# Two attention stages: half of the scaling of each head's probabilities goes from VectorE to ScalarE

## The reference

```python
s = jnp.einsum('...gnqd,...nkd->...gnqk', qb, kc, preferred_element_type=jnp.float32) * SCALE
s = jnp.where(mask, s, -jnp.inf)
m = jnp.max(s, axis=-1)
...
p = jnp.exp(s - m[..., None])
den = jnp.sum(p, axis=-1)
...
o = jnp.einsum('...gnqk,...nkd->...gnqd', p, vc.astype(jnp.float32)) / den[..., None]
```

## Time and profile before

| | |
|---|---|
| time, median of 3 runs | 998.2 us (994.24, 998.2, 1003.98) |
| span of the profiled execution | 996.8 us (its own time is not given apart from the span) |
| PE busy | 913.4 us (92%) |
| DVE busy | 655.8 us (66%) |
| ACT busy | 493.0 us (49%) |
| POOL busy | 81.1 us (8%) |

### The profile page before, as it was taken

How to read it: one execution, slowest core, us unless ns; L and a number is a source line. 1 busy time by engine, 2 the same in 40 slices (tenths; PEclk the granted TensorE clock), 3 DMA queues, 4 the chain that set the end, 5 groups by cost and what they waited for, 6 DMA issues and landing times. The chain is left out here.

```text
span 996.8 us, 14710 instructions
## 1 busy us (share of the span) xinstructions
PE 913.4 (92%) x5572; PEld 774.3 (78%) x5572; DVE 655.8 (66%) x1221; ACT 493.0 (49%) x902; POOL 81.1 (8%) x87
## 2 busy tenths in 40 slices
PE   4897779999999999999999999998988789889887
PEld 3785447899998878776799999886887468668755
DVE  4778994655555458876755556447876947787454
ACT  5444662545454335476554555334544635455651
POOL 2000000000000000000000000004643000220010
PEclk9998979999999999999999999999998999999799
DMA  9464003566656647523656656657752026533101
GB/s 332 141 204 168 1 1 113 163 190 191 192 189 210 189 152 216 174 94 107 177 171 189 200 173 212 190 154 199 242 177 95 1 69 201 169 106 118 52 1 43
DMA packets 96790, 148.69 MB, mean 149 GB/s; under 512 B 6272, under 2 KB 59680, under 8 KB 96592
## 3 DMA queue, kind: packets, MB, share of 16 engines
q1 hardware_dynamic: 94512, 140.50, 44.8%
q10 hardware_dynamic: 1296, 4.83, 1.5%
q0 software_dynamic: 912, 2.41, 0.9%
HBM read 146.67 MB, written 1.05 MB: 148 GB/s over the span
## 5 line engine op out<-in xcount | busy, mean ns | idle before, releaser
L1025 DVE TENSOR_TENSOR w_lo<-w_raw,w_hi 128x1024 fp32r<-128x1024 f32 (+2 forms) x269 | 319.9, 1211 | 139.3 <-ACT w_hi L618 135.7
L618 ACT ACTIVATE w_hi<-w_raw 128x1024 fp32r<-128x1024 f32 (+2 forms) x269 | 274.4, 1042 | 152.6 <-DMA w_raw<-in_w_gate_up 61.4
L1731 PE MATMUL ps<-hT_hi,w_lo 128*128 128x256 f32 x704 | 199.6, 284 | 2.5 <-DVE w_lo L1025 1.9
L1732 PE MATMUL ps<-hT_hi,w_hi 128*128 128x256 f32 x704 | 199.2, 283 | 0.0
L1733 PE MATMUL ps<-hT_lo,w_hi 128*128 128x256 f32 x704 | 199.2, 283 | 0.0
L1731 PE MATMUL ps<-w_hi,hT_lo 128*128 128x512 f32 (+3 forms) x448 | 174.2, 389 | 11.1 <-DVE w_lo L1025 4.4
L1733 PE MATMUL ps<-w_lo,hT_hi 128*128 128x512 f32 (+3 forms) x448 | 170.4, 380 | 0.0
L1732 PE MATMUL ps<-w_hi,hT_hi 128*128 128x512 f32 (+3 forms) x448 | 170.1, 380 | 0.0
L1731 PEld LDWEIGHTS ps<-hT_hi,w_lo 128*128 128x128 f32 x704 | 135.1, 192 | 3.2 <-ACT z L687 2.1
L1732 PEld LDWEIGHTS ps<-hT_hi,w_hi 128*128 128x128 f32 x704 | 135.1, 192 | 0.0
L1733 PEld LDWEIGHTS ps<-hT_lo,w_hi 128*128 128x128 f32 x704 | 135.1, 192 | 0.0
(11 more groups left out here) (239 smaller groups left out, 1189.6 us busy)
## 6 DMA issues: line engine op xcount, KB each, us to landing
w_raw<-in_w_gate_up SPq DMA_DIRECT2D x176, 256.0 KB, 4.4
w_raw<-in_w_down SPq DMA_DIRECT2D x44, 512.0 KB, 4.2
w_raw<-in_w_in_e SPq DMA_DIRECT2D x38, 512.0 KB, 4.7
w_raw<-in_w_qkv_o SPq DMA_DIRECT2D x24, 512.0 KB, 4.3
w_raw<-in_w_in_o SPq DMA_DIRECT2D x20, 512.0 KB, 3.7
w_raw<-in_w_out_e SPq DMA_DIRECT2D x16, 512.0 KB, 4.9
w_raw<-in_w_out_o SPq DMA_DIRECT2D x16, 512.0 KB, 3.5
w_raw<-in_w_in_e SPq DMA_DIRECT2D x8, 268.0 KB, 2.7
```

What stands on the lines that cost most here:

```text
L618: n.activation(w_hi[:, u % RING, 0:size], w_raw[:, u % RING, 0:size], ACT.Copy).then_inc(hi_ready, 1)
L1025: v.tensor_tensor(w_lo[:, u % RING, 0:size], w_raw[:, u % RING, 0:size], w_hi[:, u % RING, 0:size].bitcast(F32), ALU.subtract).then_inc(lo ...
L1731: m.matmul(o, lhs[1], rhs[0], start=start, stop=False)
L1732: m.matmul(o, lhs[0], rhs[0], start=False, stop=False)
```

## The change

In `attn0` and `attn2` DVE no longer scales tile 0. It increments a new semaphore `fac_ready`, with an instruction of its own, once `fac` is written, and scales tile 1 as before. ACT scales tile 0 of head `s-1` in step `s`, behind the exponents of head `s`, with a copy whose scale is the column of `fac`, and signals `half_ready`. The transposes of a head wait for `probs_ready` and `half_ready`. `attn1` and `attn3` are left as they are: their own functions on ACT and PE do not take part, and `scale_probs` keeps L1264 for them.

```diff
@@ ScalarE, attention, behind the exponents of head s
+                j = s - 1
+                if 0 <= j < len(inst):
+                    i, w = i0 + j, P if inst[j]["causal"] else T
+                    act.wait_ge(sem("fac_ready"), (i if stage == "attn0" else len(INST["attn0"]) + j) + 1)
+                    n.activation(prob[:, i % 4, 0:w], prob[:, i % 4, 0:w], ACT.Copy, scale=fac[:, i, 0:1])\
+                     .then_inc(sem("half_ready"), 1)
                 j = s - LAG
@@ VectorE, scale_probs
             w = P if it["causal"] else T
-            v.tensor_scalar(prob[:, i % 4, 0:w], prob[:, i % 4, 0:w], fac[:, i, 0:1], None, ALU.mult)
+            if stage in ("attn0", "attn2"):
+                dve.sem_inc(sem("fac_ready"), 1)
+            else:
+                v.tensor_scalar(prob[:, i % 4, 0:w], prob[:, i % 4, 0:w], fac[:, i, 0:1], None, ALU.mult)
             v.tensor_scalar(prob[:, i % 4, 256:512], prob[:, i % 4, 256:512], fac[:, i, 1:2], None, ALU.mult)\
              .then_inc(probs_ready, 1)
@@ TensorE, transposed
             pe.wait_ge(probs_ready, i + 1)
+            if stage in ("attn0", "attn2"):
+                pe.wait_ge(sem("half_ready"), (i if stage == "attn0" else len(INST["attn0"]) + j) + 1)
```

## The result

The changed kernel takes 1006.3 us (median of 20 runs, 1000.9 to 1010.4), the kernel before on the same chips 1002.7 us (20 runs, 994.2 to 1005.7). The ratio is 1.0047, with a 95% interval of 1.0028 to 1.0065: about 4.7 us slower, where 0.6 us faster was forecast. The 8.7 us between the forecast of 997.6 and the measured 1006.3 have three parts: 4.5 are the kernel before itself, whose median over 20 runs lies above the 998.2 of the three runs shown ahead; 3.6 are the change, by the medians; 0.6 is the gain that did not come.

What follows compares the result with a forecast made beforehand. DVE was taken as the bound in most of attn0 and in attn2 from about head 6; -0.9 us for attn0 and +0.3 for attn2 gave -0.6, so 997.6 us, with a range of 992.8 to 1003.

Steps and rivals of the forecast that it cites:

- What bounds the kernel now: DVE's list bounds attn0 except at the start (4.42 us a pair), and attn2 from about head 6 until the last four.
- What DVE is spared: Scaling of tile 0 leaves DVE: 24 x 0.20 us in attn0 and 16 x 0.26 in attn2, 9.0 us.
- What DVE is given: The separate increment costs DVE about 0.11 us, 40 times: 4.4 us, leaving a net saving of 4.6 us.
- What ACT is given: Scaling copies on ACT of 0.40 us in attn0 and 0.49 in attn2, 17.4 us in all; ACT does not become the bound.
- What becomes later: Transposes in attn0 start 2.02 us into a head, 0.47 later; a pair saves 0.18 at full clock, loses 0.13 at half.
- Sum for `attn0`: Start +0.25 us, ten pairs -1.5 with one at half clock, end +0.4: together -0.9 us.
- Sum for `attn2`: Start +0.79 us, heads 4 to 12 save 1.2, some 0.6 of latency in the last four heads: +0.3 us.
- Rival B: PE stays at half clock; some seven more pairs of attn0 each lose 0.31 to 1 us: 1002 us, chance 0.15.
- Total: Whole kernel: -0.9 + 0.3 = -0.6 us, 996.2 against the profiled 996.8, so 997.6 for the median of runs.
- nothing downstream moves: Behind the changed stages no time changes: the next projection's weight units are ready two steps ahead, no DMA issue moves.
- A: DVE's saving lands whole: -9.0 us, 989.2; with the increment's price and only the latency hidden -4.6, 993.6; chance 0.11.
- C: Latency bounds every pair of attn2: 0.71 us for each of 8 pairs, +4.8 us in total, 1003; chance 0.08.

Runs made afterwards that it cites:

- the folded kernel: The changed kernel with the fac_ready increment put on the last instruction that writes fac, everything else the same; ratio 0.9991 to the kernel before.
- the earliest transposes, between the exponents: The changed kernel with the increment on fac's last instruction and ACT scaling tile 0 of head s-1 between head s's two exponents; ratio 1.0008 to the kernel before.

## Why the prediction was wrong

**"What bounds the kernel now", "What DVE is spared", "What DVE is given": right.** A pair of `attn0` saves 0.16 to 0.17 us in the trace (4.42 to 4.26; over all the pairs that DVE paces 0.15 to 0.17) for the 0.18 forecast; a pair of `attn2` 0.29 (5.04 to 4.75) for 0.30, in the two pairs from head 8 to 12. From head 6 to 8 it is 0.15. The increment costs 0.11 us, measured by itself.

**"What ACT is given", "What becomes later": right in a pair.** The new rows last 0.39 and 0.50 us, ACT is no bound, and the transposes begin 2.05 us into the head for 2.02. One thing was off by 0.05 us: from ACT's end to PE's start it takes 0.10 us, where I carried over the 0.05 from DVE's end to PE's start.

**"Sum for `attn0`", "Sum for `attn2`": the ends right in latency, wrong in clock.** +0.4 for the end of `attn0` was 0.38 at equal clock. The last four heads of `attn2` were given +0.7 in two parts (from -0.4 to +0.3); 0.31 from head 12 to 15 and 0.42 in the tail make 0.73. The start of `attn0`, +0.25, was 0.38 from head 0 to 4 (7.39 to 7.77 us), at half clock in both. But "by the trace's clock one of them at half clock" assumed that the changed kernel would meet the clock of the one profile I had. It did not. In the profiled execution the tail of `attn0` grew by 2.4 us and that of `attn2` by 2.0, of which 2.0 and 1.5 are half clock; the pair before the tail of `attn0` lost 0.42 instead of gaining 0.18. Over four profiles a side the tails grew by 1.4 and 1.9. The terms for the ends, +0.4 and +0.6, are the ones that were too small: this is the step that failed. Rival B's mechanism came true, in places that I had not looked at. Why the clock falls there is not explained by it.

**Rival B** put the price on seven pairs inside `attn0`, decided by a PEclk below 0.75, and was given 0.15. PEclk of `attn0` only went from 0.81 to 0.76 (means over four profiles: 0.80 to 0.77), and the pairs in the middle kept their saving. The loss was in the tails, where one clock level costs the whole chain of transposes, copy and values, in single pairs at half clock near both ends of `attn0` (4.83 for 4.41, 5.61 for some 4.5), and beyond them in dense products, which PE bounds. I had also said why B was not my forecast: PE's total idle time shrinks. In `attn0` it did not grow much (57.3 - 42.9 = 14.4 us before, 15.1 after), and the clock fell all the same. The Trainium skill, "TensorE: Matmul & The Clock Gate", Part 1, ties the clock to PE's idleness; the runs with PE kept busy agree, with 62.9 us at half clock down to 45.3. A total over the stage did not tell; what would have, no run shows.

**"Total", "nothing downstream moves".** The output projection behind `attn0` waits for no weight unit in either kernel, but the clock moved, and the 45 us behind `attn0` went from 1.0 to 3.9 us at half clock, which costs 2 us each time (35.0 to 37.0).

**The size.** At equal clock the change measures +1.2 ± 0.4 us where the sum said -0.6. The 0.30 us for a us at half clock is an average over all places; in dense products and in a tail it is more (1.5 us in the tail of `attn2`, for 2 x 0.22 x 7.78 = 3.4 us at half clock). If the extra half-clock time lies in such places, as the four profiles suggest, a price near 0.45 makes 11.5 us worth 5.2, and the rest -0.6, the same as the forecast. That is an argument, not a measurement, and one result speaks against it: by the same price the folded kernel stands at -0.6 too, so that 40 increments would cost nothing at equal clock, where the increment alone comes to 2.4. How the 4.6 us divide between clock and latency is known to about 1.5 us.

**What stays open.** Why PE falls to half clock more often with the change. It is not the last head's transposes (1.0055 without them), and it is tied to the increment in some way (62.3 us at half clock without it, 74.4 with), yet the earliest transposes, between the exponents, brought it back to 71.4. With errors of 2.4 to 3.1 us on each of these means, only the gap between 62.3 and 74.4 lies clearly outside them. The increment alone doesn't bring the half-clock time (64.4). And a full clock in both tails, with filler, left 1.0038. One rule for all of these I don't have. Rivals A and C are settled: A in full needs the increment to be free, and it is not, and with the increment paid it needs the later transposes to be hidden, and at the ends they are not; C wants a loss in every pair of `attn2`, and the pairs from head 6 to 12 gained 0.15, 0.29 and 0.29.

**The base.** 4.5 of the 8.7 us came from taking three runs (994.2 to 1004.0) for the kernel's median. My range had room for the rivals only, not for that. (I also set the span of the profiled execution, 996.8, against times; in the later runs a time lies 1.8 us above its span, so part of the "1.4 above" is that. The forecast does not hang on it: 998.2 less 0.6 is 997.6 either way. And the copy with 1.1 us of DVE work behind it, in what speaks against rival C, is L1191, not L1273.)

## What to carry to other kernels

Where a stage is a chain between engines with TensorE waiting in between, count its granted clock as one of the things that the change moves: compare half-clock time over many runs, not in one profile, and look for the bill in the tails and in the dense products that follow. Put a hand-over increment on the instruction that makes the data, not beside it: here 40 separate ones turned a change with no effect into a loss of 0.5%. In this kernel work taken off the busy engine paid only where the next engine in the chain did not get its input later and TensorE was kept busy with extra matmuls in its waits (0.9936 with both, 1.0008 and 1.0001 with either alone).

## What the runs showed of the hardware

- A semaphore increment as its own instruction on VectorE takes 0.11 us of its queue: pairs of heads 0.22 us longer (4.42 to 4.64), and some 2.7 us for 40 of them in the whole kernel, by the estimate at equal clock.
- From the end of a ScalarE instruction to the matmul that waits for it: 0.10 us (109.52 to 109.62), twice the 0.05 of VectorE (108.76 to 108.81).
- A us at half clock costs this kernel 0.30 us on average (2 us for the 4.2 at the start of the dense products behind `attn0`, nothing seen in pairs that DVE paces at 4.41 us), and a run has 45 to 76 us of it by kernel. Much of the 10 us that executions of one kernel differ by goes with it: among the runs of the changed kernel, 0.973 of full speed took 1000.9 us and 0.956 took 1010.2, though 0.963 once took 1010.4.
- 120 idle transposes of 128 columns, with the kernel before, raised the mean clock of the whole kernel from 0.9685 to 0.977.
